# Four raw buffers for the expert blocks of the second dense half, and table loads ahead of block loads

## The reference

```python
def peer(h, p):
    ...
    gates = jax.nn.softmax(top_s.astype(F32), axis=-1).astype(h.dtype)
    eu, ev = p['expert_u'], p['expert_v']
    def block(args):
        xb, ib, gb = args
        act = jax.nn.gelu(jnp.einsum('nd,nhkd->nhk', xb, eu[ib]))
        return jnp.einsum('nhk,nhkd->nd', act * gb, ev[ib])
    ...
```

## Time and profile before

| | |
|---|---|
| median of 3 runs | 3881.05 us (3873.75 to 3908.81) |
| profiled execution | 3899.01 us, span 3897.2 us |
| granted TensorE clock, mean | 0.921 |
| PE / PEld / DVE / ACT / POOL busy | 84 / 73 / 64 / 37 / 22% of the span |
| HBM read, written | 769.16 MB, 40.37 MB |

### The profile page before, as it was taken

One profiled execution on the slowest core, in us unless ns is written; L12 is line 12 of the kernel. 1 busy time (PEld: TensorE's weight loads), 2 busy tenths in 40 slices (PEclk: granted clock), 3 DMA queues, 4 the chain that ended last, 5 costly groups with the idle time before them and its releaser, 6 DMA issues.

```text
span 3897.2 us, 52996 instructions
## 1 busy us (share of the span) xinstructions
PE 3262.4 (84%) x19560; PEld 2849.3 (73%) x19560; DVE 2496.6 (64%) x3095; ACT 1433.9 (37%) x1763; POOL 875.7 (22%) x469
## 2 busy tenths in 40 slices
PE   7979998769999995969966656799997888888886
PEld 2338998658888894959966656699996666666665
DVE  6985442374555535357987676677776777777776
ACT  6874333333334313343333333233332333333333
POOL 0000000010110002015654434211112333333332
PEclk9999999979999966989988878899998999999998
DMA  9973323100000001324456676899998888888885
GB/s 383 421 316 108 129 97 130 53 4 3 5 3 3 3 2 44 125 97 141 147 178 214 235 239 228 297 384 364 355 350 348 334 334 336 332 336 335 336 336 236
DMA packets 207375, 810.66 MB, mean 208 GB/s; under 512 B 81472, under 2 KB 101056, under 8 KB 118336
## 3 DMA queue, kind: packets, MB, share of 16 engines
q1 hardware_dynamic: 170432, 541.14, 37.7%
q0 software_dynamic: 36864, 268.45, 17.4%
HBM read 769.16 MB, written 40.37 MB: 208 GB/s over the span
## 4 chain that ended last, share of the span: by engine, by line
DMA 23%; DVE 16%; issue 8%; PE 4%; ACT 2%; POOL 1%; SPq 1%; DVEq 0%; ACTq 0%; POOLq 0%
DMA work<-act_table 13%; DMA raw<-expert_u 6%; DMA x<-u_rows,idx 4%; DVE x L2082 3%; DVE x L2071 2%; DVE wlo L2110 2%; ACT whi L1742 1%; PE ps L1554 1%; DVE hlo L2128 1%; DVE work L2145 1%; PE ps L1555 1%; PE ps L1556 1%; DVE work L2039 1%; DVE wlo L1543 1%; SPq L1629 1%
## 5 line engine op out<-in xcount | busy, mean ns | idle before, releaser
L1554 PE MATMUL ps<-hhi,whi 128*128 128x256 f32 x2048 | 593.3, 290 | 39.9 <-DVE wlo L2110 22.7
L1555 PE MATMUL ps<-hlo,whi 128*128 128x256 f32 x2048 | 583.6, 285 | 0.0
L1556 PE MATMUL ps<-hhi,wlo 128*128 128x256 f32 x2048 | 582.6, 284 | 0.0
L1898 PE MATMUL ps<-whi,hhi 128*128 128x512 f32 x1024 | 424.9, 415 | 155.2 <-DVE wlo L2150 134.9
L1931 POOL DMA_INDIRECT work<-expert_v,idx x128 | 341.6, 2669 | 559.8 <-DVE work L2145 541.7
L1763 ACT ACTIVATE whi<-raw 128x2048 fp32r<-128x2048 f32 x126 | 241.6, 1918 | 527.8 <-PE ps L1900 335.0
L1554 PEld LDWEIGHTS ps<-hhi,whi 128*128 128x128 f32 x2048 | 398.1, 194 | 49.2 <-issue 27.4
L282 PE MATMUL ps<-hhi,whi 128*128 128x384 f32 x1056 | 358.1, 339 | 78.6 <-DVE hlo L1413 42.9
L1899 PE MATMUL ps<-wlo,hhi 128*128 128x512 f32 x1024 | 416.2, 406 | 0.0
L1900 PE MATMUL ps<-whi,hlo 128*128 128x512 f32 x1024 | 414.9, 405 | 0.0
L1555 PEld LDWEIGHTS ps<-hlo,whi 128*128 128x128 f32 x2048 | 397.9, 194 | 0.0
(11 more groups left out here) (297 smaller groups left out, 6428.2 us busy)
## 6 DMA issues: line engine op xcount, KB each, us to landing
raw<-expert_u SPq DMA_DIRECT2D x128, 1024.0 KB
raw<-expert_v SPq DMA_DIRECT2D x128, 1024.0 KB
z<-w_ada SPq DMA_DIRECT2D x72, 1024.0 KB, 15.4
raw<-w_in SPq DMA_DIRECT2D x50, 1024.0 KB, 4.8
raw<-w_ada SPq DMA_DIRECT2D x24, 1024.0 KB, 14.6
raw<-w_out SPq DMA_DIRECT2D x16, 1024.0 KB, 4.8
raw<-w_query SPq DMA_DIRECT2D x16, 1024.0 KB
act_table<-act_f SPq DMA_DIRECT2D x128, 128.0 KB
```

The source lines that it names most:

```text
L1554: pe.matmul(bank, whi[:, r, k, :], moving_hi, start=(k == 0), stop=False)
L1555: pe.matmul(bank, whi[:, r, k, :], moving_lo, start=False, stop=False)
L1556: last = pe.matmul(bank, wlo[:, r, k, :], moving_hi, start=False, stop=(k == KD - 1))
L1898: pe.matmul(bank, ah, vh[:, part], start=first, stop=False)
```

## The change

The two halves of `done_tok` serve as third and fourth raw buffer while the second dense half runs. Each of the four has a semaphore of its own, `v_landed`. Block b goes to buffer b mod 4; `whi` and `wlo` stay at two. A block load is issued when the low half of the block four before it is done. In SyncE's loop the table loads of a period stand ahead of its two block loads. Blocks 2 and 3 are loaded ahead of the reload of `x`, and the last two blocks' loads, which stood behind the loop, are inside it now.

```diff
--- before.py
+++ after.py
@@ -1507,6 +1507,7 @@
         accs = carve(fb_, D)
         vg = [carve(fb_, D) for _ in range(4)]
         done_tok = carve(fb_, 2, D)
+        v_raw = [raw[:, 0], raw[:, 1]] + [done_tok[:, r].rearrange("p (k c) -> p k c", k=KD) for r in range(2)]
         hflat = hhi[:, :, :].rearrange("p k t -> p (k t)")
         lflat = hlo[:, :, :].rearrange("p k t -> p (k t)")
         act_hi = hflat[:, 0:2 * 2 * LAT].rearrange("p (r e t) -> p r e t", r=2, e=2)
@@ -1530,6 +1531,7 @@
         stage_out = [sem("stage_out0"), sem("stage_out1")]
         ug_landed, ug_used = [sem("ug_landed0"), sem("ug_landed1")], sem("ug_used")
         vg_landed, vg_used = [sem(f"vg_landed{r}") for r in range(4)], sem("vg_used")
+        v_landed = [sem(f"v_landed{r}") for r in range(4)]
         gate_landed = [sem("gate_landed0"), sem("gate_landed1")]
         gated_, act_high, act_split = sem("act_gated"), sem("act_high"), sem("act_split")
         weights_in, weights_ready = sem("weights_in"), sem("weights_ready")
@@ -1573,10 +1575,11 @@
                     if m < M_PRE:
                         kind, n = mix_of(m)
                         load(m, r, (w_query if kind == "q" else expert_u)[n])
-                    elif m < M_DOWN:
+                    else:
                         load(m, r, expert_u[m - NQ])
-                    else:
-                        load(m, r, expert_v[m - M_DOWN].rearrange("i (k c) -> i k c", k=KD))
+
+                def load_v(b, r):
+                    sp.dma_start(v_raw[r], b.rearrange("i (k c) -> i k c", k=KD)).then_inc(v_landed[r].sem, 16)
 
                 def spill(g):
                     sp.wait_ge(u_out.sem, g + 1)
@@ -1618,7 +1621,11 @@
                 with sp.Fori(0, REST // 4 - 1) as it:
                     rest(it)
                 for n in range(4):
-                    load_fixed(M_DOWN - 2 + n)
+                    if n < 2:
+                        load_fixed(M_DOWN - 2 + n)
+                    else:
+                        sp.wait_ge(w_low[n % 2].sem, M_DOWN // 2)
+                        load_v(expert_v[n - 2], n - 2)
                     spill(NK - 5 + n)
                 spill(NK - 1)
                 for r in range(2):
@@ -1633,24 +1640,23 @@
 
                 groups(0, 0)
                 groups(1, 2)
+                load_v(expert_v[2], 2)
+                load_v(expert_v[3], 3)
                 sp.wait_ge(ug_used.sem, SLOTS)
                 sp.wait_ge(x_saved.sem, 16)
                 sp.dma_start(x[:, :, :], x_kept).then_inc(x_back.sem, 16)
 
-                def down(it, more=True):
+                def down(it):
                     for n in range(4):
-                        r = n % 2
-                        sp.wait_ge(w_low[r].sem, it * 2 + (M_DOWN // 2 + 1 + n // 2))
-                        load(None, r, expert_v[bass.ds(it * 4 + (2 + n), 1)].rearrange("o i (k c) -> (o i) k c", k=KD))
-                        if n % 2 == 1 and more:
+                        if n % 2 == 0:
                             j = n // 2
                             sp.wait_ge(act_split.sem, it * 2 + (j + 1))
                             groups(j, it * 4 + (2 * j + 4))
+                        sp.wait_ge(w_low[n % 2].sem, it * 2 + (M_DOWN // 2 + 1 + n // 2))
+                        load_v(expert_v[bass.ds(it * 4 + (4 + n), 1)].rearrange("o i d -> (o i) d"), n)
 
                 with sp.Fori(0, NK // 4 - 1) as it:
                     down(it)
-                for n in range(2):
-                    load_fixed(M_DOWN + NK - 2 + n)
                 for k in range(0, KD, 4):
                     sp.wait_ge(added_back.sem, 3 * (k // 4 + 1))
                     sp.dma_start(y_out[:, k:k + 4, :], x[:, k:k + 4, :]).then_inc(stores_y.sem, 16)
@@ -1732,17 +1738,21 @@
                     gelu(m + 1, g + 1)
                     high_of(act, m + 3)
 
-                def rest(it):
+                def rest(it, last=False):
                     for n in range(4):
                         r = n % 2
                         act.wait_ge(prod.sem, it * 4 + (M_REST + n + 1))
                         act.wait_ge(spilled[r].sem, it * 32 + 16 * (U_REST // 2 + n // 2))
                         nc.scalar.activation(act_f[:, r], ps[:, 2 + r, 0:LAT], ACT.Gelu_apprx_tanh).then_inc(u_out.sem, 1)
-                        act.wait_ge(w_landed[r].sem, it * 32 + (16 * (M_REST // 2 + 1 + n // 2) + 16))
+                        if last and n >= 2:
+                            act.wait_ge(v_landed[n - 2].sem, 16)
+                        else:
+                            act.wait_ge(w_landed[r].sem, it * 32 + (16 * (M_REST // 2 + 1 + n // 2) + 16))
                         nc.scalar.activation(whi[:, r], raw[:, r], ACT.Copy).then_inc(w_high.sem, 1)
 
-                with act.Fori(0, REST // 4) as it:
+                with act.Fori(0, REST // 4 - 1) as it:
                     rest(it)
+                rest(REST // 4 - 1, last=True)
 
                 act.wait_ge(gated_.sem, 1)
                 act.wait_ge(prod.sem, M_DOWN)
@@ -1758,9 +1768,10 @@
                             act.wait_ge(prod.sem, it * 4 + (M_DOWN + 2 * j))
                         nc.scalar.activation(act_hi[:, (j + 1) % 2], act_in[:, (j + 1) % 2], ACT.Copy).then_inc(act_high.sem, 1)
                         for e in range(2):
-                            act.wait_ge(w_landed[e].sem, it * 32 + (16 * (M_DOWN // 2 + 1 + j) + 16))
+                            r = (2 * j + 2 + e) % 4
+                            act.wait_ge(v_landed[r].sem, it * 16 + (16 * j + 16 if j else 16))
                             act.wait_ge(prod.sem, it * 4 + (M_DOWN + 2 * j + e + 1))
-                            nc.scalar.activation(whi[:, e], raw[:, e], ACT.Copy).then_inc(w_high.sem, 1)
+                            nc.scalar.activation(whi[:, e], v_raw[r], ACT.Copy).then_inc(w_high.sem, 1)
 
                 period(0, 0)
                 period(0, 1)
@@ -2147,7 +2158,7 @@
 
                 def v_low(it, j, e):
                     dve.wait_ge(w_high.sem, it * 4 + (M_DOWN + 2 * j + 2 + e + 1))
-                    nc.vector.tensor_tensor(wlo[:, e], raw[:, e], whi[:, e].bitcast(F32), ALU.subtract).then_inc(w_low[e].sem, 1)
+                    nc.vector.tensor_tensor(wlo[:, e], v_raw[(2 * j + 2 + e) % 4], whi[:, e].bitcast(F32), ALU.subtract).then_inc(w_low[e].sem, 1)
 
                 def period(it, j, first=False):
                     lower(it, j + 1)
```

## The result

| | before | changed |
|---|---|---|
| median | 3894.93 us (4 runs) | 3728.88 us (4 runs, 3716.84 to 3737.52) |
| ratio, 95% interval | | 0.9575 [0.9511, 0.9639] |
| profiled execution, span | 3899.01, 3897.2 us | 3716.84, 3715.0 us |
| period of the second dense half | 14.0 us | 11.3 us |

The medians are 166 us apart. I had forecast 124 us less and a time of 3757 us. The sign, the place and the order of the two waits were right, the size of one term was not.

The account below looks back on a forecast made before the run. Late table loads in the second dense half set its 14.0 us period, a block-load loop close behind; 62 x (14.0 - 12.0) = 124 us less, giving 3757 us, own range 3732 to 3794, 8 in 10 range 3705 to 3830.

Parts of the forecast that it names:

- Tables ahead of blocks: Second dense half, SyncE's queue: tables get 16.2 us of lead against 7.7 needed, so VectorE's 234 us wait goes.
- the old loop of 14.1 us: Second half: table landing 7.72, gate product and gathered row 2.87, low half 2.29, next issue 1.2 us set the period.
- Four buffers: Second half: blocks requested four low halves ahead have 19.6 us against 8.1 needed; ScalarE's 178 us wait goes.
- the second loop: Second half: block landing 8.1, ScalarE's copy 1.92, low half 2.29, hand-overs 0.3 us make 12.6 us.
- The cost of 0 for the handshake and the wait on act_split: Second half: two-block high and low tiles and SyncE's new wait order cost nothing, with only 1 us of cover.
- The start and the end: Edges of the second half: taken as 0, bounds 3 us gained or lost at the start; nothing changes behind 3859.59.
- near 2992: Profile sign: the second low half of the first pair in the second half would still start near 2992 us.
- The DMA floor of 11.8 us, taken as 12.0: Second half: transfers become the bound; 0.84 x 14.06 = 11.8 us, divided by a 0.98 share, gives a 12.0 us period.
- Rival 1: Second half gets only the expert_u half's 353 GB/s: period 13.4, 3842 us, or 13.0, 3819 us; chance 0.14.
- Rival 2: Second half's DMA runs at its best: period 11.2 or TensorE's 10.9, gains 174 to 192 us; chance 0.14.
- Rivals 3 and 4: Slow TensorE clock stretches in each second-half period: one gives 3794 us, chance 0.06; two give 3906 us, chance 0.04.
- Rival 5: Second half's tables stay late behind block loads in the shared queue: period 13.7, 3862 us; chance 0.05.

Follow-up runs that it names:

- tables first only: Kernel before with one edit: a period's two table loads stand ahead of its two block loads, still two raw buffers; 3758.52 us, ratio 0.9655.
- half the gathers: Changed kernel with every second gather of expert_v rows left out, VectorE's work unchanged; 3688.34 us, ratio 0.9495.
- four buffers of both kinds: Changed kernel with four block buffers and four gather buffers in the first half's loop too, from its third turn; 3695.39 us, ratio 0.9516.
- extra writes: Changed kernel with a 128 KB write from SBUF to HBM behind each block load in the second half's loop; 3764.78 us, ratio 0.9676.
- four buffers in both halves: Changed kernel with four block buffers in the first half's loop too, from its third turn; 3733.91 us, ratio 0.9623.

## Why the prediction was right, and where its size was off

- **Tables ahead of blocks.** Right in kind, and the larger part: 125 of the 168.5 us (tables first only against before). That the old loop of 14.1 us was closed by the tables alone is shown from both sides, since four buffers without the move left it at 13.98. What was wrong in this step is the landing: I set the lead of 16.2 us against the landing of 7.7 of the old traffic, and the landing grew to 14.4 to 18.7.
- **Four buffers.** Right: worth something only behind the first. I had put the second loop at 12.6; it is 11.98, as the landing of a pair's first block fell from 8.2 to 7.6 us in the mean. The term was sized from a landing taken in another traffic.
- **The cost of 0 for the handshake and the wait on act_split.** Right: with fewer bytes the same code reached TensorE's own 10.87.
- **The start and the end.** 0.5 us and 0.0, inside the 3 us I had allowed. The point itself moved to 2977.94 with the 14 us of the earlier stages, so "near 2992" was no good test; the distance to the first product is.
- **The DMA floor of 11.8 us, taken as 12.0.** This is the mis-sized term. The transfers became the bound, as said, but at 11.28 us. 62 x 0.72 = 45 us is the whole difference between 124 and 168.5. The share is the summed time of the packets over that of 16 engines, so I had taken 0.84 x 14.06 = 11.8 us as the packets' time in a period and divided it by a highest share of 0.98. Two things were off. The packets' time itself nearly held: 0.98 x 11.98 = 11.7 us with tables first only, 1.02 x 11.28 = 11.5 in the changed kernel, which is 0.3 us of the 0.72. The larger part, some 0.4 us, is the highest share: it reached 1.02, and 11.8 / 1.02 is 11.6. The 0.98 came from the first half, 2520 to 2960 us, while the earlier trace rows had 1.01 at 420 and 421 GB/s, which I used only as a bound. With another mix the packets' time would have misled more: half the gathers needs 0.92 x 10.87 us for 3.67 MB, 2.7 us a MB where the kernel before has 2.5. Why a packet takes longer in one mix than in another stays open.
- **Rival 1,** 353 GB/s and by the Trainium skill ("DMA: Bandwidth & Descriptors", section "Where 436 GB/s comes from") 358 for HBM to SBUF. Out here, where one core streams: 417 GB/s were held for 661 us, all of it loads and gathers. The 353 was a ring of the first half's own, gone with four buffers of both kinds.
- **Rival 2** had the price right, 174 us at 11.2; what happened is much nearer to it (166) than to my forecast. I gave it 0.14 for want of a reason why the tables' 2 KB rows should not cost; 417 GB/s with the tables in it show that they don't cost much, and extra writes in 1 KB rows cost only their bytes. It was also the rival whose cause, a deep queue at its best rate, is nearest to what happened: by the mechanism the runs favour it over my forecast.
- **Rivals 3 and 4,** slow stretches of the clock: none, 1.00 in every 20 us from 3003 to 3663. TensorE is busy 97% of the time there, so the holes of 9% that I had expected did not occur; with holes of 7% (606.62 of 650 us, tables first only) the clock was 0.99.
- **Rival 5,** the tables still late: the mechanism is there in part. They take up to 18.7 us to land and VectorE waits 50.5 us for them, where I had said near 0. Since the transfers bind, something has to wait: with half the gathers this wait is gone, and the period falls only by the 0.4 us down to TensorE's own. The Trainium skill, "DMA: Bandwidth & Descriptors", says in "Queues, rings and completion order" that each ring is taken in its own order. The landing grown from 7.7 to over 14 us behind more blocks agrees; no run here parts that from the gathers' share of the same engines.

What stays open: why the timed runs of the changed kernel spread over 21 to 42 us and those with four buffers in both halves over 11 to 13. The rate of the first half from 2520 to 2680 us lay between 363 and 386 GB/s in nine profiles of the same code, so its two-deep rings are a likely cause, but that was not tested apart.

## What to carry to other kernels

Close the loops on paper: landing + converts + the wait to the next issue, for each load that is waited for, and rank them; only the longest pays, and a shorter one's remedy is worth nothing until the longest is gone. The DMA share times the period gives the packets' time, and for an unchanged mix it held within 3% here (11.8, 11.7, 11.5 us); but take the highest share and rate from the fastest stretch with transfers of the same kind, even if it lasts 20 us, and not from one that may wait in a loop of its own. And when one operand comes early, look at what the engine now does sooner, and whom that holds up: here VectorE's low half against GpSimd's gather.

## What was not expected of the hardware

- Mixed block loads, table loads and gathers held 417 GB/s for 661 us, nearly as much as plain weight loading (421).
- 131 KB writes in rows of 1 KB, two a period, cost their bytes (0.26 MB, 0.59 us) and nothing beyond.
- GpSimd needs 0.94 us to issue a gather while VectorE is idle (38 of 38 from 2680 to 2920 us before) and 2.4 to 2.8 us where one of VectorE's 2.3 us operations has been running for 0.35 to 0.73 us (120 of 120 from 3000 to 3846 us before): it ends about 0.8 us behind that operation. In the changed kernel a low half that began less than 0.05 us before the gather did not hold it up; at 0.05 us or more it did (84 of 84):

```profile
3319.44 0.94 POOL L1942 DMA_INDIRECT work<-expert_v,idx  x1 [2.32 <-DVE work L2156]
```

```profile
3319.43 2.33 DVE L2161 TENSOR_TENSOR wlo<-raw,whi 128x2048 fp32r<-128x2048 f32 x1 [0.27 <-ACT whi L1774]
```

- The DMA share can be 1.00 while TensorE is the bound and gets everything in time (240.00 of 240 us at 385 GB/s).
